# VectorE's order at the entry into the out projection, and token sums of the first pass and of the tail on GpSimd

## What is computed

```python
h = rmsnorm(x, norm_g) * (1 + scale) + shift
z = h @ w_in                      # q, k, v, gate_a, ranks, u, gate_b, mg_a, mg_b
...                               # gated linear attention both ways, Fourier mixing
y_a = o @ w_proj_a
y_b = four @ w_proj_b
merged = sigmoid(mg_a) * y_a + sigmoid(mg_b) * y_b
x = x + gate * (merged @ w_out)
y = rmsnorm(x, final_norm_g)
```

## Time and profile before

| what | value |
|---|---|
| median of 3 runs | 1928.45 us (1926.27 to 1932.30) |
| the profiled execution's own time | 1932.9 us |
| its span, first to last instruction | 1931.1 us |
| mean granted TensorE clock | 0.990 |
| busy: TensorE, VectorE, ScalarE, GpSimd | 97%, 63%, 49%, 33% |

### The profile page before, as it was taken

How to read it: one execution, slowest core, us unless ns; L and a number is a source line. 1 busy time by engine, 2 the same in 40 slices (tenths; PEclk the granted TensorE clock), 3 DMA queues, 4 the chain that set the end, 5 groups by cost and what they waited for, 6 DMA issues and landing times.

```text
span 1931.1 us, 30194 instructions
## 1 busy us (share of the span) xinstructions
PE 1871.2 (97%) x10393; PEld 1750.0 (91%) x10393; DVE 1208.0 (63%) x2112; ACT 941.4 (49%) x1961; POOL 640.7 (33%) x671
## 2 busy tenths in 40 slices
PE   7899999999999999999999998999999999998997
PEld 2899999999999999999999996888898899996886
DVE  4978877785444435644444454666656567578787
ACT  4565667653445446444455324777742142243343
POOL 0136634034334512334333000000842024342644
PEclk9999999999999999999999999999999999999998
DMA  7578878967898989779788968655456766785443
GB/s 287 210 270 276 294 277 318 378 242 268 275 327 293 313 314 356 233 236 294 256 280 274 348 206 337 247 218 194 184 208 213 229 204 222 245 286 181 163 164 131
DMA packets 174817, 494.78 MB, mean 256 GB/s; under 512 B 15120, under 2 KB 72906, under 8 KB 164300
## 3 DMA queue, kind: packets, MB, share of 16 engines
q1 hardware_dynamic: 160844, 442.53, 66.5%
q10 hardware_dynamic: 13824, 50.34, 6.5%
HBM read 323.98 MB, written 159.39 MB: 250 GB/s over the span
## 4 chain that ended last, share of the span: by engine, by line
PE 72%; DVE 9%; DMA 7%; POOL 4%; issue 4%; ACT 3%; SPq 1%; ACTq 0%; DVEq 0%; POOLq 0%
PE bank L2576 46%; PE bank L2922 5%; PE bank L2876 5%; DMA x_st<-in_x 3%; PE bank L2740 3%; PE bank L2707 3%; PE bank L2805 2%; PE bank L2718 2%; PE bank L2729 1%; PE bank L2520 1%; POOL h_lo L1165 1%; POOL yt L1303 1%; DVE me_op L2215 1%; POOL yt L1300 1%; DVE me_s L2348 1%
## 5 line engine op out<-in xcount | busy, mean ns | idle before, releaser
L2576 PE MATMUL bank<-h_hi,w_op 128*128 128x384 f32 x4032 | 1051.4, 336 | 15.0 <-ACT outs L1382 4.7
L2576 PEld LDWEIGHTS bank<-h_hi,w_op 128*128 128x128 f32 x4032 | 731.8, 188 | 21.0 <-issue 21.0
L2576 PE MATMUL bank<-h_lo,w_op 128*128 128x384 f32 x2016 | 675.0, 335 | 0.0
L2576 PEld LDWEIGHTS bank<-h_lo,w_op 128*128 128x128 f32 x2016 | 379.5, 188 | 0.0
L1870 DVE TENSOR_TENSOR w_op<-w_raw,w_op 128x512 fp32r<-128x512 f32 x240 | 189.3, 789 | 90.1 <-ACT w_op L1342 87.3
L1190 POOL TENSOR_TENSOR decs<-decs,qk_s 128x192 f32<-128x192 f32 x192 | 128.3, 706 | 326.8 <-ACT decs L1416 326.5
L1342 ACT ACTIVATE w_op<-w_raw 128x512 fp32r<-128x512 f32 x240 | 149.2, 623 | 158.4 <-PE bank L2576 155.8
L2955 PE MATMUL bank<-ow_op,me_op 128*128 128x512 f32 x756 | 177.3, 395 | 7.6 <-DVE u4o L2427 3.8
L2955 PEld LDWEIGHTS bank<-ow_op,me_op 128*128 128x128 f32 x756 | 143.5, 191 | 41.2 <-issue 5.7
L2922 PE MATMUL bank<-op_a,a_op 128*128 128x384 f32 x1008 | 174.9, 334 | 0.0
L2922 PEld LDWEIGHTS bank<-op_a,a_op 128*128 128x128 f32 x1008 | 174.6, 188 | 0.1
(11 more groups left out here) (274 smaller groups left out, 2844.8 us busy)
## 6 DMA issues: line engine op xcount, KB each, us to landing
w_op<-wt_dram SPq DMA_DIRECT2D x192, 512.0 KB, 5.8
wt_dram<-w_op ACTq DMA_DIRECT2D x96, 512.0 KB, 4.7
w_raw<-in_w_in SPq DMA_DIRECT2D x48, 768.0 KB, 6.4
w_raw<-in_w_in SPq DMA_DIRECT2D x24, 1024.0 KB, 6.9
qk_dec<-decs SPq DMA_DIRECT2D x48, 384.0 KB, 6.6
mg_dram<-outs SPq DMA_DIRECT2D x24, 768.0 KB, 7.6
swap<-qk_s SPq DMA_DIRECT2D x48, 192.0 KB, 5.9
v_dram<-outs SPq DMA_DIRECT2D x24, 384.0 KB, 4.9
```

The costliest lines, as they stand in the source:

```text
L2576: ins = pe.matmul(bnk, w_op[slot][:, part, k, :], h[:, j, k, :], start=(first and k == 0 and part == 0 and h is h_hi), stop=(k == HK - 1 a ...
```

## The change

Three things are changed, and SyncE issues one load elsewhere:

- In pass 0 of the in projection GpSimd makes the sums `s2`, `s1` and the second `s1`, in halves of 768 columns, and VectorE only `a21-a11`.
- At the end of the a projection VectorE splits the out projection's operands 2, 1 and 3 and finishes the last four merge tiles between them; operands 5 and 6 come behind the first sums of the out projection. `load_ow(6)` moves from the seventh to the fifteenth merge tile of the last pass.
- In the last block GpSimd multiplies `u2o` by the gate and adds the residual for two quarters (`scaled_sum` of VectorE before); VectorE's other instructions close up, and the counts `END` on `s_ad` become smaller.

```diff
-        END = {"u2": AD + 1, "u4": AD + 2, "t22": AD + 4, "22": AD + 6, "t12": AD + 8, "t21": AD + 10, "11": AD + 12,
-               "12": AD + 14, "21": AD + 16}
+        END = {"u2": AD + 1, "u4": AD + 2, "t22": AD + 4, "22": AD + 6, "11": AD + 8,
+               "12": AD + 10, "21": AD + 12}
@@ sync
-                    elif at == 6:
+                    elif at == 14:
                         load_ow(6)
@@ gpsimd
+            a11, a12, a21, a22 = (h32[:, r, HK * c:HK * c + HK, :] for r in range(2) for c in range(2))
+            pool.wait_ge(s_ha0, 6)
+            pool.wait_ge(s_hv0, 6)
+            pool.wait_ge(s_s, 1)
+            sum_parts(s2, a22, a21, ALU.add)
+            pool.wait_ge(s_s, 2)
+            sum_parts(s1, s2, a11, ALU.add)
+            pool.wait_ge(s_hl, 5)
+            sum_parts(s1, a12, s2, ALU.subtract)
@@ gpsimd, at its end
+            pool.wait_ge(s_ad, END["u2"])
+            for u, sl in enumerate((slice(512, D), slice(0, 512))):
+                y = yt[FINAL % 2][u][:, sl]
+                pool.wait_ge(s_yst[u], 16 * (FINAL - 1))
+                pool.tensor_tensor(y, u2o[:, :], res_gate[:, 1, sl], ALU.mult).then_inc(s_add, 1)
+                pool.wait_ge(s_add, 4 * FINAL + 2 * u + 1)
+                pool.wait_ge(s_xin[u], 16 * NM)
+                pool.tensor_tensor(y, y, x_end[u][:, sl], ALU.add).then_inc(s_add, 1)
@@ vector, pass 0
-            first_sum(1, s2[:, :, :], a22, a21, ALU.add)
-            first_sum(2, s1[:, :, :], s2[:, :, :], a11, ALU.add)
-            dve.wait_ge(s_hl, 5)
-            first_sum(3, s1[:, :, :], a12, s2[:, :, :], ALU.subtract)
@@ vector, a projection
-                if step + 1 < NPROD * NA:
-                    low_op(step + 1)
+                if step + 1 == NPROD * NA:
+                    break
+                low_op(step + 1)
...
-                    elif i == 6:
-                        for j in (2, 1):
-                            low_me(0, j)
-                        sum_me(0, 3)
-                        low_ow(3)
                 merge(step, 2)
+
+            for j in (2, 1):
+                low_me(0, j)
+            sum_me(0, 3)
+            low_ow(3)
+            merge(NPROD * NA - 1, 0)
+            low_me(0, 3)
+            merge(NPROD * NA - 1, 1)
+            low_ow(4)
+            merge(NPROD * NA - 1, 2)
+            low_me(0, 4)
             merge(NPROD * NA - 1, 3)
-            low_me(0, 3)
-            low_ow(4)
-            for j in (4, 5):
-                low_me(0, j)
-            low_ow(5)
-            low_me(0, 6)
@@ vector, block loop of the out projection
                 else:
-                    low_ow(6)
+                    low_me(0, 5)
+                    low_ow(5)
                 add_quarter(b, 1)
                 if b == 0:
                     add_quarter(b, 2)
+                    low_me(0, 6)
+                    low_ow(6)
@@ vector, last block
-            scaled_sum(y[0][:, sl[1]], u2o[:, :], 0, 1, END["22"])
-            scaled_sum(y[1][:, sl[0]], u2o[:, :], 1, 0, END["t12"])
+            end_quarter(0, 0, 0, 4, x_end[0][:, sl[0]], END["22"])
             scale_rows(FINAL - 1, 1)
-            end_quarter(0, 0, 0, 4, x_end[0][:, sl[0]], END["t21"])
+            dve.wait_ge(s_add, 4 * FINAL + 2)
             end_quarter(0, 1, 2, 5, y[0][:, sl[1]], END["11"])
+            dve.wait_ge(s_add, 4 * FINAL + 4)
             end_quarter(1, 0, 3, 6, y[1][:, sl[0]], END["12"])
```

## The result

| | time, us | against before |
|---|---|---|
| before, median of 6 runs | 1928.86 (1926.27 to 1932.3) | |
| changed, median of 6 runs | 1936.78 (1934.91 to 1942.73) | ratio 1.0045, 95% interval 1.0029 to 1.0061 |
| changed, profiled execution | 1937.04, span 1935.2, clock 0.99 | before 1932.9, span 1931.1 |

What follows compares the result with a forecast made beforehand. TensorE, busy 97% of the span, was taken as the bound, with VectorE alone setting the tail's end. 4.4+4.9-0.1=9.2 us on the median 1928.45 gave 1937.7 us, range 1929 to 1944.4.

Steps and rivals of the forecast that it cites:

- Part A: In projection's first window: three first sums on GpSimd make low part 5 end 4.4 us later, all reaching TensorE.
- the walk: First window, GpSimd and VectorE alternating instruction by instruction: third sum ends at 71.8, low part 5 at 75.0.
- Part B: Out projection's entry: the late load of operand 6 delays `p1o` and product 4; +4.9 us, bounds +1.5 to +7.7.
- The next block begins today at 1756.35+7.33=1763.7: +3.1: Out projection: the next block starts after sums and a low part at 1766.8, against 1763.7 today, +3.1 us.
- 1.8 of clock: Out projection: a TensorE wait costs clock; 24 matmuls took 7.33 us instead of 5.5, 1.8 a gap.
- Part C: Tail: VectorE loses four instructions of 0.69 us but alternates with GpSimd's four; -0.1 us, bounds -2.9 to +1.3.
- The reorder's gain arrives: Out projection's entry: operand 6's load is issued by 1737.5, so products 4 to 6 run on; total +1.2 us; chance 0.16.
- The DMA wait stays: Out projection's entry: the 2.89 us DMA wait at the `mg_a` multiplication remains; +7.7 there, total +12.0 us; chance 0.15.
- GpSimd's sums run beside VectorE: First window and tail: no lock between the engines; -1.0 and -2.9 us there, total +1.0 us; chance 0.08.
- the 5.46: Out projection's entry: a 1 MB load into an idle queue takes 5.46 us from issue to use.

Runs made afterwards that it cites:

- the order alone: Against the kernel before, only the new order at the out projection's entry and `load_ow(6)` at the fifteenth merge tile: 1936.9 us, ratio 1.0037.
- the load at tile 7: Against the kernel before, the change's order at the out projection's entry, load of operand 6 left at the seventh merge tile: 1929.23 us, ratio 1.0004.
- the run with whole instructions: Against the kernel before, the three first sums on GpSimd, each one instruction of 1536 columns: 1930.59 us, ratio 1.0007.
- the load of operand 6 at tile 12: Against the kernel before, the change's order at the out projection's entry, that load behind the twelfth merge tile's store: 1928.78 us, ratio 0.9997.
- input 6 early: The kernel with operand 6's load at tile 12, plus input 6's low part ahead of operand 5's: 1924.42 us, ratio 0.9971 against the kernel before.

## Why the prediction was right, and where not

**Part A, +4.4: mechanism right, 0.5 too long.** By the profile it is 3.85, by the run of it alone 2.9 (1.2 to 4.8). Counted from the modulated tiles, the walk had the first sum at 1.3 (1.4 seen), the second's end at 12.5 (12.05), the third's at 21.1 (20.5), the low part's start at 22.6 (22.04): each of the two turns in contention ends a few tenths early. That all of it reaches TensorE in the first pass is shown by the matmul behind `soft`, 3.86 later. That all of it reaches the end is likely but shown only within the interval.

**Part B, +4.9: each position right, the price read off the wrong one.** Against the start of the out projection (1734.23 before, 1732.90 after):

| | predicted | seen |
|---|---|---|
| load of operand 6 issued | 11.4 | 11.3 |
| `p1o` ends | 19.3 | 19.1 |
| load of the next block issued | 24.6 | 24.6 |
| taken up | 30.1 | 30.1 |
| next block starts | 32.6 | 32.8 |

The sum is right to 1.2 us. The step that failed is the last, "The next block begins today at 1756.35+7.33=1763.7: +3.1", with 1.8 of clock. The end does not hang on the start of TensorE's second block, which came 3.3 later, but on the load's taking up: 30.12 for 24.06, +6.1 (+6.5 against the mean of 23.6 above), and with the rest at 172.8 all of that reaches the end (the order alone: 29.29, +5.2, and by time +7.1, 5.0 to 9.5). Both timelines show the way from there. `yt` of the second block, the last thing that TensorE waits for ahead of the tail, starts 1784.78-1763.02=21.76 behind the taking up in the changed kernel. In the kernel before it was 1780.07-1758.29=21.78, and TensorE waited for it too:

```profile
1780.07 0.69 DVE L2427 TENSOR_TENSOR yt<-bank,u4o 128x512 f32<-128x512 f32 x1
...
1780.90 19.29 PE L2955 MATMUL bank<-ow_op,me_op 128*128 128x512 f32 x84 [0.91 <-DVE yt L2427]
```

Between lie the block's sums and low parts, the gate rows, GpSimd's residual sums, ScalarE's squares and the row scaling, each in its engine's fixed order. The chain of waits of the changed kernel runs over them, and not over TensorE (pieces of the view, from the load on):

```profile
1757.52 5.48 DMA me_ld<-me_dram
...
1768.69 2.35 DVE res_gate L2476 x2
...
1771.82 2.68 POOL yt L1309
...
1774.58 2.74 POOL yt L1312
...
1777.34 1.16 ACT junk L1782 x2
...
1780.67 0.68 DVE u4o L2441
```

The chain of the kernel before, from which the prediction read its block start, named TensorE's 24 matmuls. Behind them it goes on with VectorE's gate rows at 1763.96, and VectorE's own low parts end at 1764.05: the two ways there were a tie, and the view shows one of them.

Gaps or slow matmuls of TensorE ahead of the wait for `yt` are swallowed by waits whose end TensorE does not set. The 24 matmuls behind the gap took 7.15 us for 5.5 at full clock, and TensorE then stood 2.93 us for the second block's `me_op`. So the 1.8 that the prediction added for clock cost nothing here.

**Part C, -0.1: right in kind.** The rest is 0.6 shorter, and the instructions that wait for the other engine are there.

**Sum.** 3.85+6.1-0.6=9.3 for 9.2, since A was 0.5 too dear, B 1.2 too cheap and C 0.5 short of its gain. That the errors cancel to 0.1 is luck, and so is part of B itself: without the 1.8 of clock, for which there was no place, it would have been 3.1. That the profiled execution is only 4.1 longer comes from stretches with the same code: the middle was 3.55 shorter and the modulated tiles 1.63 earlier.

**The rivals.** "The reorder's gain arrives" fell on the point it named: the load was issued 11.3 behind the start of the out projection, not 3.3 (its 1737.5). "The DMA wait stays" fell: no wait at 1729.89; with the load at tile 7 it is back. "GpSimd's sums run beside VectorE" fell by the low part of 2.90 for 1.75 and by the run with whole instructions.

**The two 1 MB loads.** Issued 1744.22 and used 1749.64, issued 1757.52 and used 1763.02: 5.4 and 5.5 us, as the 5.46 of the earlier trace rows. In the kernels with the load of operand 6 at tile 12 that load took 7.2 to 8.1 from issue to use, so the 5.46 does not hold at every place in the queue. The Trainium skill's fit for one DMA on GpSimd's path ("DMA: Bandwidth & Descriptors", the anatomy of one DMA) gives an estimated 4.4 for each, and by it B would have been 2.1 less. These loads, from SyncE's queue, took longer; the trace decides for the row.

Left open: why the middle varies by 5.6 us between executions, which of GpSimd and VectorE goes first when both stand ready, and why the times put the loss of the order (7.1) and the gain of input 6 early (5.0 against the kernel without it) above the segments (5.2 and 3.7), though within their intervals.

## What to carry to other kernels

Before pricing a shift, look for the mark from which the time to the end is the same over variants, and price the shift of that mark. In this kernel a gap of TensorE that opened or closed ahead of the mark was worth nothing, because a chain over four engines held its next wait. And ask what stands behind a wait in each engine's queue. A 2 us copy of an operand needed two products later cost 6.7 us by the times (5.2 by the segments), because the copy that freed a bank stood behind it. One low part of 0.7 us, moved ahead of one of 2.3, lengthened a gap of TensorE by 0.6, but released a load earlier and gave 3.7 by the segments and 5 by the times.

## What was not expected

- The rest of 172.8 us is the same within 0.12 in ten kernels, while the middle of 1663 us varies by 5.6.
- Longer instructions on one of two engines that exclude each other can end sooner: sums as whole instructions had the last low part 0.65 us earlier than as halves, though VectorE's 0.7 us subtraction took 2.93.
- GpSimd takes 3.48 us for one sum of 1536 columns, and 1.85 for each half.
